# Decoder step with differential attention: the query norm goes into the exponential's row scale, its sums of squares are taken by groups of 32 columns, and four key row blocks get places of their own

## The reference, cut to what matters

```python
k, v = split(h @ w_kv)                       # 8 heads, 2 key maps of 64, values of 128
k = rms_norm(k, k_norm)                      # per head and map, over 64 numbers
q = rms_norm(h @ w_q, q_norm)                # likewise: y * rsqrt(mean(y*y) + eps) * gain
...
s = einsum('qhmd,khmd->hmqk', q, k) * 64**-0.5     # two maps m for each head
p = softmax(where(causal, s, -inf))
w = p[:, :, 0] - lam * p[:, :, 1]
o = einsum('hqk,khd->qhd', w, v)
```

## Time and profile before

| | |
|---|---|
| median of 3 runs | 2011.28 us |
| the profiled execution | 2011.12 us |
| its span, first to last instruction | 2009.3 us |
| PE busy | 1844.4 us, 92% |
| DVE, ACT, POOL busy | 786.1, 717.5, 148.8 us |
| chain that ended last | PE 76%, DMA 8%, DVE 7%, ACT 3% |

### The profile page before, as it was taken

The page is one execution under the profiler, slowest core; times in us unless marked ns, Lnnn a source line. Parts: engine busy times, 40 slices in busy tenths (PEclk is TensorE's granted clock), DMA queues, the critical chain, the costliest instruction groups (busy, mean ns, idle before and its releaser), DMA issues.

```text
span 2009.3 us, 43320 instructions
## 1 busy us (share of the span) xinstructions
PE 1844.4 (92%) x17559; PEld 1669.9 (83%) x17559; DVE 786.1 (39%) x1414; ACT 717.5 (36%) x1094; POOL 148.8 (7%) x287
## 2 busy tenths in 40 slices
PE   4898879899999999899998999999788899999998
PEld 2483679799999999899996777776478899999997
DVE  6566423343332233422753545454323433323232
ACT  1524233343333322322525555555111433333212
POOL 2000011210000012100101000000023100000000
PEclk8579989899999999899989999999769899999999
DMA  8758752222222222222137899998722122222222
GB/s 247 252 178 271 252 153 84 63 63 81 80 81 83 68 86 81 69 78 81 31 117 256 309 381 378 373 374 317 256 92 74 53 84 82 79 80 66 82 83 76
DMA packets 245008, 301.08 MB, mean 150 GB/s; under 512 B 10188, under 2 KB 195472, under 8 KB 244816
## 3 DMA queue, kind: packets, MB, share of 16 engines
q1 hardware_dynamic: 241752, 290.22, 43.7%
q0 software_dynamic: 2016, 5.67, 0.8%
q10 hardware_dynamic: 1120, 3.44, 0.5%
HBM read 291.92 MB, written 7.37 MB: 149 GB/s over the span
## 4 chain that ended last, share of the span: by engine, by line
PE 76%; DMA 8%; DVE 7%; ACT 3%; issue 3%; SPq 3%; POOL 0%; ACTq 0%; DVEq 0%; POOLq 0%
PE ps L583 57%; PE ps L506 5%; DMA kpg<-in_cache_k 3%; PE ps L533 2%; DMA raw<-in_w_ada_mix 2%; PE ps L820 2%; PE ps L962 2%; DMA raw<-in_w_ada_ffn 1%; PE ps L722 1%; SPq L455 1%; SPq L462 1%; PE ps L891 1%; PE ps L918 1%; PE ps L874 1%; DMA vpg<-in_cache_v 1%
## 5 line engine op out<-in xcount | busy, mean ns | idle before, releaser
L583 PE MATMUL ps<-hr,ws 128*128 128x288 f32 x5760 | 780.5, 298 | 28.9 <-DVE hr L1749 17.2
L583 PEld LDWEIGHTS ps<-hr,ws 128*128 128x128 f32 x5760 | 775.8, 190 | 31.9 <-issue 24.2
L1743 DVE TENSOR_TENSOR ws<-raw,ws 128x1024 fp32r<-128x1024 f32 x200 | 235.3, 1178 | 697.9 <-ACT ws L1230 697.9
L1230 ACT ACTIVATE ws<-raw 128x1024 fp32r<-128x1024 f32 x200 | 201.4, 1010 | 631.9 <-PE ps L583 631.6
L583 PE MATMUL ps<-gr,ws 128*128 128x288 f32 x2112 | 279.4, 294 | 0.0
L583 PEld LDWEIGHTS ps<-gr,ws 128*128 128x128 f32 x2112 | 279.1, 188 | 0.0
L1367 ACT ACTIVATE kTs<-ps 128x512 f32<-128x512 f32 x256 | 139.6, 597 | 156.8 <-PE ps L506 156.7
L506 PE MATMUL ps<-ident,kpg 128*128 128x128 f32 x1024 | 140.2, 281 | 11.4 <-DMA kpg<-in_cache_k 7.4
L506 PEld LDWEIGHTS ps<-ident,kpg 128*128 128x128 f32 x1024 | 113.1, 143 | 38.4 <-issue 20.5
L533 PE MATMUL ps<-raw,cond 128*32 128x256 f32 x896 | 84.9, 488 | 44.7 <-DMA raw<-in_w_ada_mix 36.7
L583 PE MATMUL ps<-hg,ws 128*128 128x288 f32 x768 | 105.2, 300 | 8.9 <-DVE ws L1743 8.9
(11 more groups left out here) (325 smaller groups left out, 1653.1 us busy)
## 6 DMA issues: line engine op xcount, KB each, us to landing
kpg<-in_cache_k SPq DMA_DIRECT2D x128, 512.0 KB, 5.7
vpg<-in_cache_v SPq DMA_DIRECT2D x128, 512.0 KB, 5.9
raw<-in_ffn_w SPq DMA_DIRECT2D x88, 512.0 KB, 3.8
raw<-in_w_ada_mix SPq DMA_DIRECT2D x48, 512.0 KB, 5.4
raw<-in_w_ada_ffn SPq DMA_DIRECT2D x48, 512.0 KB, 4.7
raw<-in_ffn_w SPq DMA_DIRECT2D x48, 384.0 KB, 3.4
raw<-in_w_ada_kv SPq DMA_DIRECT2D x16, 512.0 KB, 5.4
raw<-in_ssm_w_glu SPq DMA_DIRECT2D x16, 512.0 KB, 4.2
```

The costliest lines, as they stand in the source:

```text
L583: return mm(ps[:, 4 * s + 2 * tile + h, 0:HALF], ws[:, (u * S + j) % 2, w, k, :], src[:, k0 + k, v, h * HALF:(h + 1) * HALF], start=(k0 + ...
L1230: A(ws[:, w, 0, 0:nk, :].rearrange("p k n -> p (k n)"), raw[:, slot, 0:nk, :].rearrange("p k n -> p (k n)"), ACT.Copy).then_inc(slab_high, 1)
L1743: TT(f(ws[:, w, 1, 0:nk, :]), f(raw[:, slot, 0:nk, :]), f(ws[:, w, 0, 0:nk, :]).bitcast(F32), ALU.subtract).then_inc(raw_done[slot], 1)
```

## The change

Four things change together.

1. The gain of the query norm is multiplied in when ACT copies q out of PSUM. 1/root of the prompt's tokens is no longer multiplied into `qT`: since the scores have the query token on the partitions, it is given to the exponential as a scale by row (`scaleq`), and to the negated maximum (`minusq`). Only the 64 sample columns of `qT` are still multiplied, by one DVE operation after 16 small matmuls for all heads.
2. The sums of squares are made with the squares as the moving side: 16 matmuls of 32 mask columns as weights, each into its own 32 partitions (four heads to a bank), 288 moving columns. ACT copies the result to `t1`, and 10 matmuls with `t1` as weights and 8 columns of the identity turn it so that tokens are on the partitions.
3. Key blocks 0 to 3 get `krow`, four places of their own; the sample's keys and values get one buffer of `tok` each. ACT copies blocks 0 to 4, 6 and 8, DVE blocks 5, 7 and 9.
4. POOL builds `tri`, `qn` and the small masks at the start of the stretch, and the first sequence's queries before it starts the transfers of the values. PE waits for the last rows' copies only after the first scores.

```diff
+    krow = share("krow", [P, QB, D], 16 * KB)
-    rootq = t2[:, 0, 0:H * 5 * 2].rearrange("p (n m) -> p n m", m=2)
+    NQ = H * 5 * 2
+    rootq, scaleq, minusq = (t2[:, 1, n * NQ:(n + 1) * NQ] for n in range(3))
...
+        def root_column(h, i, m):
+            return ((h // 4 * 5 + i) * 4 + h % 4) * 2 + m
+        def row_place(n):
+            v, i = n // (QB + 1), n % (QB + 1)
+            if i == QB:
+                return tok[0:DB * DS, v, :]
+            return vtok[:, i].rearrange("p h d -> p (h d)") if v else krow[:, i]
...
PE:
-            pe.wait_ge(free[0], USES["qtok"][0])
+            for s in range(2):
+                pe.wait_ge(free[s], USES["qtok"][s])
             pe.wait_ge(sqq_ready, H)
-            token_sums(sqq, blockd[:, 0:P:P // 4], 0)
+            for a_ in range(2):
+                for half in range(2):
+                    for g in range(4):
+                        last = mm(ps[32 * g:32 * g + 32, 4 * a_ + half, 0:HALF], blockd[:, 0:P:4], sqq[:, 4 * a_ + g, half * HALF:(half + 1) * HALF],
+                                  start=True, stop=True)
+                last.then_inc(sums_full, 1)
             pe.wait_ge(head_ready, 2 + H)
-            for n in range(QB):
+            for n in range(2):
+                token_rows(n)
+            pe.wait_ge(sums_copied, 2)
+            for a_ in range(2):
+                for i, at in enumerate(FIVE):
+                    c = (a_ * 5 + i) * 8
+                    last = mm(ps[:, 4, c:c + 8], t1[:, a_, at:at + P], ident[:, 0:P:P // 8], start=True, stop=True)
+            last.then_inc(sums_full, 1)
+            for n in range(2, QB + 1):
                 token_rows(n)
             pe.wait_ge(root_ready, 1)
-            pe.wait_ge(free[1], USES["qtok"][1])
             for h in range(H):
-                if h >= 2:
-                    pe.wait_ge(head_ready, 2 + H + h - 1)
-                spread(4 * (h % 2), lambda i: [rootq[:, h * 5 + i, m:m + 1] for m in range(2)])
-                if 0 < h < H - 1:
-                    token_rows(QB - 1 + h)
-            pe.wait_ge(head_ready, 2 + 2 * H - 1)
-            for s in range(2):
-                pe.wait_ge(free[s], USES["attn"][s])
+                for m in range(2):
+                    c = root_column(h, QB, m)
+                    last = mm(ps[m * DK:(m + 1) * DK, 5, h * DK:(h + 1) * DK], rootq[:, c:c + 1].to_broadcast([P, DK]), ident[:, P // 2:],
+                              start=True, stop=True)
+            last.then_inc(spread_full, 1)
+            for n in range(QB + 1, 2 * (QB + 1)):
+                token_rows(n)
...
                     if keys:
                         scores(b, par, u)
+                    if b == 0 and u == 0:
+                        for s in range(2):
+                            pe.wait_ge(free[s], USES["attn"][s])
...
ACT:
-                            A(by_halves(qT, i * per + u), ps[:, 4 * s:4 * s + 2, 0:HALF], ACT.Copy)
+                            A(by_halves(qT, i * per + u), ps[:, 4 * s:4 * s + 2, 0:HALF], ACT.Copy, scale=vec[:, 121:122])
...
-            act.wait_ge(sums_full, 1)
             act.wait_ge(head_ready, 2 + H)
-            A(rootq, ps[:, 0, 0:H * 20:2].rearrange(...), ACT.Sqrt, bias=eps[:, 0:1], scale=1.0 / DK).then_inc(root_full, 1)
-            for i in range(QB + 1):
-                s = i % 2
-                wait_unit(act, "qtok", s, i // 2)
-                if i >= 2:
-                    act.wait_ge(tok_put[s], 16 * (i // 2))
-                A(tok[0:NTOK[i], s, :], ps[...], ACT.Copy).then_inc(free[s], 1)
+            for a_ in range(2):
+                act.wait_ge(sums_full, a_ + 1)
+                A(halves(t1[:, a_, :]), ps[:, 4 * a_:4 * a_ + 2, 0:HALF], ACT.Copy).then_inc(sums_copied, 1)
+            row_out(0)
+            row_out(1)
+            act.wait_ge(sums_full, 3)
+            A(rootq, ps[:, 4, 0:NQ], ACT.Sqrt, bias=eps[:, 0:1], scale=1.0 / DK).then_inc(root_full, 1)
+            for n in (2, 3, 4, 6, 8):
+                row_out(n)
...
-                    done = A(e01[:, m, 0:w], ps[:, 2 + m, 0:w], ACT.Exp, bias=l01[:, par, 2 + m:3 + m], scale=SCALE,
+                    done = A(e01[:, m, 0:w], ps[:, 2 + m, 0:w], ACT.Exp, bias=l01[:, par, 2 + m:3 + m], scale=scaleq[:, c + m:c + m + 1],
...
POOL (order only: tri, qn, pick, sign; then the transfers of rows 0 to 4):
+            for n in range(QB + 1):
+                store_rows(n)
+            pool.wait_ge(head_ready, HEADS)
+            new_keys(0, 0)
+            for n in range(QB + 1, 2 * (QB + 1)):
+                store_rows(n)
+            for b in range(1, NBUF):
                 new_keys(b, b)
             for s in range(2):
                 pool.wait_ge(tok_put[s], 16 * (6, 4)[s])
+            nc.gpsimd.memset(mark[:, 9:10], 0.0).then_inc(v_used, 4)
...
DVE:
             REC(rootq, rootq).then_inc(root_ready, 1)
-            for h in range(H):
-                head_scale(qT, h, 4 * (h % 2), vec[:, 121:122], h)
-                ... (rows 5 to 9 copied in between)
+            dve.wait_ge(root_ready, 1)
+            TS(scaleq, rootq, SCALE, None, ALU.mult)
+            step(TS(minusq, rootq, -SCALE, None, ALU.mult))
+            dve.wait_ge(spread_full, 1)
+            TT(qT[:, :, SEQ:T], qT[:, :, SEQ:T], ps[:, 5, :].rearrange("p (h t) -> p h t", h=H), ALU.mult).then_inc(head_ready, 1)
+            for n in (5, 7, 9):
+                ... (wait for the row block, copy it to row_place(n))
...
-                TS(l01[:, par, 2:4], l01[:, par, 0:2], -SCALE, None, ALU.mult).then_inc(s_max, 1)
+                c = root_column(h, i, 0)
+                TT(l01[:, par, 2:4], l01[:, par, 0:2], minusq[:, c:c + 2], ALU.mult).then_inc(s_max, 1)
```

More of the change, by code:

```diff
@@ L181, in spare @@
         return mark[:, c:c + 1]
+    HEADS = 3 + H
     over = place[0]
@@ L1027, in _ @@
                 if h >= 2:
-                    pe.wait_ge(head_ready, 2 + 2 * H + h - 1)
+                    pe.wait_ge(head_ready, HEADS + h - 1)
                 spread(4 * (h % 2) + 2, lambda i: [rooto[:, h * 5 + i:h * 5 + i + 1]])
@@ L1332, in _, with row_out @@
             dense("q", tail=False)
-            act.wait_ge(sums_full, 1)
             act.wait_ge(head_ready, 2 + H)
-            A(rootq, ps[:, 0, 0:H * 20:2].rearrange("p (n m) -> p n m", m=2), ACT.Sqrt, bias=eps[:, 0:1], scale=1.0 / DK).then_inc(root_full, 1)
-            for i in range(QB + 1):
-                s = i % 2
-                wait_unit(act, "qtok", s, i // 2)
-                if i >= 2:
-                    act.wait_ge(tok_put[s], 16 * (i // 2))
-                A(tok[0:NTOK[i], s, :], ps[0:NTOK[i], 4 * s + 2:4 * s + 4, :].rearrange("p b c -> p (b c)"), ACT.Copy).then_inc(free[s], 1)
+            for a_ in range(2):
+                act.wait_ge(sums_full, a_ + 1)
+                A(halves(t1[:, a_, :]), ps[:, 4 * a_:4 * a_ + 2, 0:HALF], ACT.Copy).then_inc(sums_copied, 1)
+            def row_out(n):
+                s, i = n % 2, n % (QB + 1)
+                wait_unit(act, "qtok", s, n // 2)
+                dst = row_place(n)
+                A(dst, ps[0:NTOK[i], 4 * s + 2:4 * s + 4, :].rearrange("p b c -> p (b c)"), ACT.Copy).then_inc(free[s], 1)
+            row_out(0)
[4 more added lines that the diff above has]
+                row_out(n)
             def block_exp(n):
-                w, par = (n % QB + 1) * P, n % 2
+                w, par, c = (n % QB + 1) * P, n % 2, root_column(n // QB, n % QB, 0)
                 act.wait_ge(s_max, n + 1)
@@ L1398, in _ @@
             for h in range(H):
-                act.wait_ge(head_ready, 2 + 2 * H + h + 1)
+                act.wait_ge(head_ready, HEADS + h + 1)
                 A(hr[:, h, 0, :], oT[:, h, :], ACT.Copy).then_inc(h_high, 1)
@@ L1534, in _, with store_rows @@
             apply("q")
-            for n in range(2 * (QB + 1)):
+            for s in range(2):
+                pool.wait_ge(free[s], USES["qtok"][s])
+            step(nc.gpsimd.memset(tri[:, :], 0.0))
+            nc.gpsimd.affine_select(out=tri[:, :], in_=tri[:, :], compare_op=ALU.is_ge, fill=MASKED, base=0,
+                                    pattern=[[-1, P]], channel_multiplier=1).then_inc(tri_ready, 1)
+            step(nc.gpsimd.memset(qn[:, :].rearrange("p b h c -> p (b h c)"), 0.0))
+            quarter = ident[:, :].rearrange("p (g c) -> p g c", c=32)
+            TT(pick[:, :].rearrange("p (g t) -> p g t", t=CH), quarter[:, :, 0:CH], quarter[:, :, CH:2 * CH], ALU.add)
+            TT(sign[:, 1:2], ones[:, 0:1], neglam[:, :], ALU.subtract).then_inc(sinit, 1)
+            def store_rows(n):
                 s, v, i = n % 2, n // (QB + 1), n % (QB + 1)
@@ L1542, in _ @@
                         (1, 1): "b t h d -> (b t) (h d)"}[(int(i == QB), v)]
[L1543 to L1559, removed]
+                pool.dma_start(rows_.rearrange(form), row_place(n)).then_inc(tok_put[i % 2], 16)
+            for n in range(QB + 1):
+                store_rows(n)
+            pool.wait_ge(head_ready, HEADS)
```

(10 more changed lines are left out.)

11 lines of the change are left out of this document (4 added, 7 removed).

## The result

| | before | after |
|---|---|---|
| median of 11 runs each | 2011.46 us | 2003.32 us |
| ratio, 95% interval | | 0.9947 (0.9928 to 0.9966) |
| the profiled execution | 2011.12 us | 2002.01 us |
| its span | 2009.3 us | 2000.2 us |
| PE busy | 1844.4 us | 1834.6 us |

The ratio is a gain of 10.7 us (0.0053 x 2011); the two medians are 8.1 us apart, the two means 11.1. The forecast was 9.7 less, with a range of 1996 to 2007. The single times scatter by some 10 us (1998 to 2011), far more than the three runs of before let expect: in the profiles the work ahead of the stretch alone ends anywhere between 1014 and 1025 us.

What follows compares the result with a forecast made beforehand. PE's 40.7 us from the sums of squares to the first scores, nearly all on the chain, was the bound; -14.9 + 3.8 - 1.5 + 1.3 + 1.6 = -9.7 us gave 2001.6 against the median, range 1996 to 2007.

Steps and rivals of the forecast that it cites:

- Start and sums: PE before the first rows: start 0.55 us later, sums of squares in 2.4 us, then a 2.1 us standstill for key scaling.
- Turning the sums: 10 matmuls on PE after the sums: 20 weight loads of 186 ns, 3.7 us at full clock.
- upper bound of 1.8: The new `spread` on PE after row 4: 32 records take at most 1.8 us.
- The expected fall: PE's clock falls by the time the sums are turned: +3.8 us, bounds 0 and some +10.
- The return during transposes: PE's clock, once fallen, returns during the row blocks; the skill's rule against this would give 2007.8 us.
- The rival of a clock that stays up: PE's clock does not fall in the stretch, so no 3.8 us: 1997.8 us; chance 0.18.
- First page and POOL: First cache page turned at 1042.6 in place of 1057.47, -14.9 us at full clock; POOL's queries ready before it.
- POOL's wait: PE's 1.50 us wait for POOL's queries at the first scores falls away: -1.5 us.
- Page loads: Page 4's load beside the last rows' transfers in the first sequence: +1.3 us, bounds 0 and 2.2.
- page loads that stall by more than 2 us in the first sequence: Sign that would show the prediction wrong, in the attention's first sequence; the page load term was +1.3 us.
- The exponential: ACT's 64 exponentials each cost about 0.1 us more; 8 of 32 blocks on the chain pay: +1.6 us.
- upper bound of 6.4: Rival where the exponentials' extra 0.1 us reaches the chain in all 32 blocks: +6.4, so 2006.4 us; chance 0.08.

Runs made afterwards that it cites:

- e0: The changed kernel run again with no edit; ratio 0.9938 (0.9914 to 0.9961) to the kernel before.
- e4: Changed kernel with POOL copying the first sequence's queries only after starting all row transfers, as before; one run, first scores 28.7 us after the last query product.
- e12: The changed kernel run once more with no edit, beside three other runs; ratio 0.9950 (0.9931 to 0.9969) to the kernel before.
- e5: Changed kernel with transfers of value blocks 5 to 8 to HBM started only after the first sequence's scores; ratio 0.9930 (0.9906 to 0.9954) to the kernel before.
- e1: Changed kernel with the old sums of squares (80 records of 4 columns); ratio 0.9986 (0.9969 to 1.0002) to the kernel before.
- e6: Kernel before with only the new sums of squares added; ratio 0.9952 (0.9935 to 0.9969) to the kernel before.
- e10: Changed kernel with two value blocks turned first (order 5, 6, 0 to 4, 7 to 9), second run; ratio 0.9919 (0.9896 to 0.9941) to the kernel before.
- e9: Changed kernel with two more one-column ACT copies between each block's two exponentials; ratio 0.9964 (0.9941 to 0.9986) to the kernel before.
- e11: Changed kernel with a constant scale in the exponential and negated maximum, second run; ratio 0.9921 (0.9904 to 0.9939) to the kernel before.

## Why the prediction was right

The direction, the size and the mechanism came out: the time lies 0.53% below before, against 0.48% forecast. That it came so near is in part luck: the first page was won by 2 to 3 us more than forecast, and page loads and exponentials gave more back.

- *Start and sums.* Pause of 2.05 us, sums in 2.18 us, then a pause of 2.42 us until the keys are scaled: forecast 1.9, 2.4 and 2.1. Right.
- *Turning the sums: mis-sized.* The step took "20 weight loads of 186 ns" as 3.7 us at full clock. Measured: 2.30 us, and 4.28 at 1.2 GHz, where the step meant 6.7. The 186 and 333 ns of the earlier trace rows are how long a load lasts, not how far apart loads are; they overlap. The earlier trace rows had the distance: 20 loads in a window of 4 us at 0.50, so 200 ns. `spread` took 1.15 us, where the upper bound of 1.8 was taken.
- *The clock.* The expected fall came in six of nine profiles and cost 4.5 us (25.1 against 20.6), for +3.8. The return during transposes was as forecast: in e0 the grant was 0.50 when PE began the rows at 1029.82 and began to rise while it did nothing but these transposes (0.71 from 1033 to 1034, 1.00 in the next us), ahead of `spread` at 1034.40. That rise speaks against what the Trainium skill says of transposes ("TensorE: Matmul & The Clock Gate", section "Part 4: PE-mode transpose"), that they don't count as work that raises the clock, as the earlier trace rows did. The fall doesn't: it too came while PE did only transposes. The rival of a clock that stays up came in one profile of the nine; in two more the fall cost nothing.
- *First page and POOL.* Forecast from the last product's end: 23.3 us with the clock up, 27.1 with it down. Measured: 20.6 and 25.1; the difference is mostly the two mis-sized items above. POOL's wait is gone, and e4 brings 1.19 us of it back.
- *Page loads.* +1.3 forecast. From the first scores to the first exponential's table load it takes 30.8, 30.4 and 31.8 us (after, e0, e12), 28.9 before: +2.1 in the mean. The place was right, and by e5 so was the cause, "beside the last rows", for pages 4 and 5; but waits on later pages remain without these rows. One of the prediction's own signs of being wrong came up here: page loads that stall by more than 2 us in the first sequence. They stall by 2.03, 1.50 and 3.17.
- *The exponential: the term that was sized too small.* The prediction charged the blocks that stood on the chain of before, "since the others end before PE gets to them". It counted 8; the 11 pieces lie in 9 blocks, so the step as meant is 1.8 in place of 1.6. In the changed kernel the chain has 13 blocks, 2.3 us at most; the profiles' mean says 3.0 (standard error 1.3), the times 5.7 (1.6), near the upper bound of 6.4. All lie above the 1.6; the size stays open. The price of one was right (89 to 91 ns, for 0.1; the Trainium skill, "ScalarE: Activation LUTs", section "What ACT_TABLE_LOAD costs", has 93). A chain shows what ended last, not how much slack the rest has: 0.18 us more on a block was enough to put four more on it.

With the measured terms the sum is -13.0 (first page, clock down; -17.5 with it up) - 1.6 (POOL) + 2.1 (page loads) and the exponentials. With 5.7 for these it is -6.8, or -11.3 with the clock up; at six to three some -8.3, against 10.1 to 12.5 measured. With 2.3 it is some -11.7, with 3.0 some -11.0. So the smaller sizes close the sum; the 2 to 4 us that 5.7 leaves open lie within the intervals, which are 7.6 to 9.5 us from end to end. The chances of the prediction add up a little differently than it says: 0.88 for faster and 0.09 for no change.

What the change is worth part by part follows from e1 and e6 within their intervals: the new sums are the larger part of the net gain. Norm in the scale, small spread, key places and POOL's order together win 8.7 us ahead of the attention and give some of it back in the exponentials and the page loads; what each of them is worth alone was only looked at for the places and the order.

## What to carry to other kernels

A factor by row that is moved into an instruction which runs 64 times is paid up to 64 times; ask what one more 0.1 us on each costs, and don't trust the chain of the kernel before to say that most are hidden, since the longer instructions can come onto it. When a long stage becomes short, look for what it had hidden: here the scaling of the keys, and an order that puts two independent row blocks into that gap brought another 6.2 us (e10 against e12). Take the distance between pipelined instructions from counts in a window, not from their durations.

## What the runs showed of the hardware

The same program has its TensorE clock fall in some executions and not in others. Of nine profiles with one opening, six show 0.50 during the first rows and the turned sums, at a cost of 4.5 us; two show a fall during the sums only, hidden under DVE's reciprocal of 3.75 us and so without cost (e9, e11); one shows none. A 128x128 float32 weight load lasted 186 ns at the least in the earlier trace rows and 190 to 192 in the turned sums, while 20 records ended in 2.30 us. Two one-column copies on ACT, recorded with 196 and 206 ns, moved what followed by 0.17 us together (e9).
